# Pre-weighted exponentials and plain transposes in a sparse attention, and a convolution's first tap on the scalar engine

## The chip, the cores and the metric

The kernel runs on one core of a Trainium2 chip. The core has a matrix engine (TensorE, PE in the profile), a vector engine (VectorE, DVE), a scalar engine (ScalarE, ACT) and a general engine (GpSimd, POOL); a fifth (SyncE, SP) issues the weight loads. Each runs its own list of instructions in order and waits on semaphores that the others raise. On-chip data lie in SBUF; TensorE writes its products to eight PSUM banks, which VectorE and ScalarE read. The metric is the device time of one execution in microseconds; lower is better.

## The reference, cut to what matters

The program is three transformer blocks on 256 tokens of width 1024. The change touches the third, in two branches that are computed side by side. One is a sparse ("native sparse") attention of 16 heads in 4 groups, whose selection and window branches both become ordinary causal attention over the 256 tokens here:

```
s = einsum("bqgrd,bkgd->bgrqk", qb, kb) - slopes[:, :, None, None] * dist
p = jax.nn.softmax(jnp.where(mask, s, NEG), axis=-1)
return jnp.einsum("bgrqk,bkge->bqgre", p, vb)
o = gates[..., 0:1] * o_cmp + gates[..., 1:2] * o_slc + gates[..., 2:3] * o_win
```

The other is a gated delta rule, whose input first goes through a causal convolution of four taps and a SiLU:

```
qkv = jax.nn.silu(causal_depthwise_conv(qkv, conv_w))   # 3 * 1024 channels, 4 taps
q = l2norm(...); k = l2norm(...)
```

## The kernel before, in words

Each engine has its own program (`tensor_program`, `scalar_program`, `vector_program`, `gpsimd_program`), written as Python loops over the same steps. `Mark` counts what an engine has finished; `wait_ge(*dve.at("conv", j))` waits until VectorE has finished step conv of tile j. The order within an engine is the order of the code; no scheduler changes it.

Every weight is split in two float32r parts for accuracy: ScalarE copies 1024 columns to `whi` (L1394), VectorE subtracts to get `wlo` (L1913), and a 1024 x 128 product takes 24 matmuls (L567 to L569). The split runs at most three units ahead, in four buffers.

The stage of the change is the projection `f2`: 24 iterations s = 0 to 23, each giving one 128-channel tile j = F2[s] of queries, keys and values of the delta rule (16 tiles of keys and queries, which also need squares for the norms, and then 8 of values, j >= 16, which are transposed). In 17 of the 24 iterations (`STEPS2`) one turn of the sparse attention goes along. Of 16 turns in all, turns 0 and 1 have their scores before the stage; iterations 1, 2, 4, 5, 7, 8, 9, 11, 12, 14, 15, 16, 18 and 19 hold the scores of turns 2 to 15. These 14 are called head iterations below.

What each engine does in iteration s before the change, in its order:

- TensorE: the scores of turn i (L1051, `ns_scores`); the product of tile s (`product`), for which the PSUM bank of tile s-2 must be free and the `wlo` of unit s ready; column sums of squares (L585) or transposes of values (L1162) of tile s-2; then the turn i-2 (L1060, `ns_turn`) and the values of turn i-3 (L1074, L1082).
- ScalarE: `whi` of unit s+3; for value tiles the copies of the transposed tile (L1754); tanh of tile s-1 (L1763) after its convolution; the square of tile s-1 (L1768) after VectorE's `conv` of s-1; four exponentials of turn i (L1691) with their sums; two copies of the turned exponentials (L1699); on every second turn a copy of the output (L1705).
- VectorE: on a head iteration the reciprocal and gate of turn i-1 (L2345, L2347, `ns_weigh`), then the four maxima of turn i (L2334) and its bias (L2339); `wlo` of unit s+3 (L1913); `conv` of s-1, the SiLU's last factor (L2427); then the convolution of tile s, four operations from PSUM that each add one tap (L2436 the first, L2439 three more, each waiting for the one before); on every second turn a subtraction for the output (L2361).
- GpSimd: for each turn the product of the identity matrix with the four weights of each row (L2669), 128 x 512, in two buffers `dg2`.

The softmax weight (gate over sum) is applied in the turn itself: the exponentials are the stationary operand and the diagonal matrix of weights the moving one, so that the product is the transposed and weighted tile. These are float32 products. The other transposes of the kernel use TensorE's transpose with the identity.

Of the kernel before, what the change touches and what calls it, by code (L numbers as in the profile page):

```python
# [9 lines left out]
ALU = mybir.AluOpType  # L10
ACT = mybir.ActivationFunctionType
# [3 lines left out]
T = 256  # L15
# [293 lines left out]
STEPS2 = [(j + 1) * (N2 + 1) // 24 - j * (N2 + 1) // 24 for j in range(24)]  # L309

F2 = (*range(8, 16), *range(8), *range(16, 24))
CUTS = ((0, 128), (128, 384))
# [10 lines left out]
def program(nc, a):  # L323
    ctx = ExitStack()
    with ctx:
        area = [ctx]

        def sb(name, shape, dt=F32):
            return area[-1].enter_context(nc.sbuf_tensor("sb_" + name, shape, dt))
# [33 lines left out]
        sq = sb("sq", [128, KT, T])  # L363
# [83 lines left out]
        close()  # L447
        ss = sb("ss", [128, 3, 2, 384])
        pt2 = sb("pt2", [128, 2, 2, 384])
        dg2 = sb("dg2", [128, 2, 4, 128])  # L450
        nst = st[:, 0:64].rearrange("p (n k u t) -> p n k u t", n=4, k=4, u=2)
        close()
        scope()
# [30 lines left out]
        def C(name, lo=0, hi=None):  # L484
            s, e = COLS[name]
            return col[:, s + lo:(e if hi is None else s + hi)]
# [56 lines left out]
        def ps_of(step):  # L543
            return bank[bank_of.get(step, 0)]
# [7 lines left out]
        def tensor_program(te):  # L552
# [500 lines left out]

            def ns_turn(i):

                P.wait_ge(*pool.at("dg2", i))
                for u in range(2):
                    ps = take(RAS, ("npt", i, u), (act, ("npt", i, u)))
                    for k in range(3):
                        end = te.matmul(ps[:, k * 128:(k + 1) * 128], ss[:, i % 3, u, k * 128:(k + 1) * 128], dg2[:, i % 2, 2 * u + (k > 0), :], start=True, stop=True)  # L1060
                    end.then_inc(*pe.up(("npt", i, u)))

            def ns_values(i):
# [312 lines left out]
        def scalar_program(sc):  # L1376
# [306 lines left out]
            def attn_head(i):  # L1683
                if i < N2:
                    aa, r, _ = PAIRS2[i]
                    x = nst[:, i % 4, :, :, :]
                    A.wait_ge(*dve.at("nsneg", i))
                    for u in range(2):
                        for t, (lo, hi) in enumerate(CUTS):
                            p = ss[:, i % 3, u, lo:hi]  # L1690
                            sc.activation(p, p, ACT.Exp, bias=x[:, 1, u, t:t + 1], scale=slope((2 * aa + u) * 4 + r), accum_out=x[:, 2, u, t:t + 1]).then_inc(*act.up(("nsexp", i, u, t)))  # L1691

            def attn_tail(i):
                if 0 <= i - 2 < N2:
                    if i - 2 >= 2:
                        A.wait_ge(*pe.at("npv", i - 4))
                    for u in range(2):
                        A.wait_ge(*pe.at("npt", i - 2, u))
                        sc.activation(pt2[:, i % 2, u, :], ps_of(("npt", i - 2, u))[:, 0:384], ACT.Copy).then_inc(*act.up(("npt", i - 2, u)))  # L1699
                if 0 <= i - 3 < N2:  # L1700
                    aa, r, e = PAIRS2[i - 3]
                    j = aa * 4 + r
                    if e == 1:
                        A.wait_ge(*pe.at("npv", i - 3))
                        sc.activation(onh[:, j, :], ps_of(("no", j))[:, 0:T], ACT.Copy).then_inc(*act.up(("onh", j)))  # L1705
# [41 lines left out]
            def f2_later(s):  # L1747
# [11 lines left out]
                if 0 <= s - 1 < 24:  # L1759
# [4 lines left out]
                    if j < 16:  # L1764
# [2 lines left out]
                            A.wait_ge(*pe.at("qks", j // 2 * 2 + 9))  # L1767
                        sc.activation(sq[:, j % 8, :], src, ACT.Square).then_inc(*act.up(("qksq", j)))  # L1768

            step = 2  # L1770
            for s in range(24):
                weights("f2")
                f2_later(s)
                if STEPS2[s]:
                    attn_head(step)
                    attn_tail(step)
                    step += 1
            f2_later(24)
# [118 lines left out]
        def vector_program(ve):  # L1897
# [531 lines left out]
            def convolve(j):  # L2429
                dst = qk[:, j, :] if j < 16 else sq[:, j % 8, :]  # L2430
                ps = ps_of(("f2", j))
                wcol = C("conv", 4 * j, 4 * j + 4)
                V.wait_ge(*pe.at("f2", j))
                if j >= 16:
                    V.wait_ge(*pe.at("qks", (j - 16) // 2 * 2 + 1))
                ve.tensor_scalar(dst, ps[:, 0:T], wcol[:, 3:4], None, ALU.mult).then_inc(*dve.up())  # L2436
                for d in range(1, 4):
                    V.wait_ge(*dve.now())
                    ve.scalar_tensor_tensor(dst[:, d:T], ps[:, 0:T - d], wcol[:, 3 - d:4 - d], dst[:, d:T], ALU.mult, ALU.add).then_inc(*dve.up(*[("f2", j)] * (d == 3)))  # L2439

            step = 2
# [179 lines left out]
        def gpsimd_program(gp):  # L2621
            G = Waiter(gp)

            def regions(before):

                G.wait_ge(*pe.at(before))
                G.wait_ge(*act.at(before))
                G.wait_ge(*dve.at(before))

            def sums(norm):  # L2630

                for k in range(1, KT - 1):
                    G.wait_ge(*act.at("sq", norm, k))
                    if k > 1:
                        G.wait_ge(*pool.at("sum", norm, k - 1))
                    gp.tensor_tensor(sq[:, 0, :], sq[:, 0, :], sq[:, k, :], ALU.add).then_inc(*pool.up(("sum", norm, k)))  # L2636


            gp.memset(one, 1.0).then_inc(*pool.up("one"))
            for i in range(N0):  # L2640
                total = st[:, 64 + 2 * i:66 + 2 * i].unsqueeze(2).to_broadcast([128, 2, 128])
                G.wait_ge(*dve.at("w", i))
                if i == 0:
                    G.wait_ge(*dve.at("ctx", 7))
                if i > 1:
                    G.wait_ge(*pe.at("pt", i - 2, 1))
                gp.tensor_tensor(dg0[:, i % 2, :, :], ident.unsqueeze(1).to_broadcast([128, 2, 128]), total, ALU.mult).then_inc(*pool.up(("dg0", i)))
            for norm in ("ffn0", "mix1", "ffn1"):
                sums(norm)
            for k in range(1, KT - 1):  # L2650
                for norm, src in (("fin", sq), ("mix2", z8)):
                    G.wait_ge(*act.at("sq", norm, k))
                    if k > 1:
                        G.wait_ge(*pool.at("sum", norm, k - 1))
                    gp.tensor_tensor(src[:, 0, :], src[:, 0, :], src[:, k, :], ALU.add).then_inc(*pool.up(("sum", norm, k)))


            regions("block1")
            gp.memset(hvx[:, :, :, :], 0.0).then_inc(*pool.up("hvx"))
            gp.memset(bk[:, :, :], 0.0).then_inc(*pool.up("bk"))  # L2660
            gp.memset(pcs[:, :, :, :], 0.0).then_inc(*pool.up("pcs"))
            pool.note("f1")
            regions("f1")
            for i in range(N2):
                x = nst[:, i % 4, 3, :, :].rearrange("p u t -> p (u t)").unsqueeze(2).to_broadcast([128, 4, 128])
                G.wait_ge(*dve.at("nw", i))
                if i > 1:
                    G.wait_ge(*pe.at("npt", i - 2, 1))
                gp.tensor_tensor(dg2[:, i % 2, :, :], ident.unsqueeze(1).to_broadcast([128, 4, 128]), x, ALU.mult).then_inc(*pool.up(("dg2", i)))  # L2669
            pool.note("f2")  # L2670
            regions("f2")


            def decay(hd):
                G.wait_ge(*act.at("decay", hd))
                gp.tensor_tensor(Ebuf[:, hd % 2, :], Ebuf[:, hd % 2, :], K("mge"), ALU.mult).then_inc(*pool.up(("E", hd)))

            def level_mask(lv, n):
                msk = K("lev", lv * 64, lv * 64 + 64).unsqueeze(1).to_broadcast([128, 4, 64])
                G.wait_ge(*dve.at("W", 2 * n + 1))  # L2680
                if lv == 1:
                    G.wait_ge(*pe.at("first", n))
                    G.wait_ge(*dve.at("Y", 0, n))
                if lv > 1:
                    G.wait_ge(*pe.at("lup", lv - 1, n))
                gp.tensor_tensor(four(Wl, n), four(Wb, n)[:, :, 0:64], msk, ALU.mult).then_inc(*pool.up(("mask", lv, n)))

            G.wait_ge(s_con2, 16)
            for hd in range(8):
                decay(hd)  # L2690
            for n in range(4):
                level_mask(0, n)
            for n in range(4):
                level_mask(1, n)
            for lv, n in LEVELS:
                if lv < 5:
                    level_mask(lv + 1, n)
            G.wait_ge(*pool.now())
            gp.memset(Ys[64:128, :, 0:64], 0.0).then_inc(*pool.up("zeros"))
            pool.note("delta")  # L2700
            sums("mlp2")
# [276 lines left out]
```

## Time and profile before

| | us |
|---|---|
| median of 3 runs | 1182.01 (1180.71 to 1186.97) |
| the profiled execution's own time | 1183.51 |
| its span in the profile | 1181.7 |
| PE busy | 1138.0 (96% of the span) |
| DVE busy | 818.8 (69%) |
| ACT busy | 591.2 (50%) |
| POOL busy | 82.1 (7%) |

A busy time is the union of an engine's instructions. Matmuls are pipelined, one of 278 ns starting about 115 ns after the one before it, so a full TensorE shows as busy without gaps, and short gaps are hidden. For VectorE and ScalarE it is the start of each instruction that tells how the order moves on. The `f2` stage lies at about 660 to 796 us of the span.

### The profile page before, as it was taken

How to read it: one execution, taken by the hardware profiler on the slowest of the kernel's cores; microseconds unless marked ns; L12 is line 12 of the kernel's file. 1: busy time of each engine (PE TensorE's matmuls, PEld its weight loads, DVE VectorE, ACT ScalarE, POOL GpSimd, SP SyncE). 2: the span in 40 equal slices, each digit the busy share in tenths (PEclk: the TensorE clock that was granted, in tenths of full speed). 3: DMA queues.
4: the chain of work that ended last, by engine and by line, in shares of the span. 5: the costliest groups of instructions: out<-in, count | busy, mean ns of one | idle time of the engine just before them, and what ended most of it. 6: DMA issues, size and time to landing. Idle time of an engine off the chain costs nothing.

```text
span 1181.7 us, 23984 instructions
## 1 busy us (share of the span) xinstructions
PE 1138.0 (96%) x10258; PEld 1077.9 (91%) x10258; DVE 818.8 (69%) x1496; ACT 591.2 (50%) x1085; POOL 82.1 (7%) x101
## 2 busy tenths in 40 slices
PE   8888799999998999999999999999999999999999
PEld 2786799999997999999989988879999999999998
DVE  6776769988886776555765788879554665877443
ACT  2545555444435544554465657653224545665432
POOL 0000010000011000011100111113500001000000
PEclk9899999999999999999998999999999999999999
DMA  9732938888882567540742423222124555855520
GB/s 389 328 143 95 369 154 338 342 341 329 328 344 104 214 229 282 204 158 31 286 150 101 144 72 108 97 83 73 39 73 143 178 185 183 311 188 205 191 82 14
DMA packets 32220, 225.36 MB, mean 191 GB/s; under 512 B 3569, under 2 KB 4721, under 8 KB 5105
## 3 DMA queue, kind: packets, MB, share of 16 engines
q1 hardware_dynamic: 30530, 221.21, 49.9%
q10 hardware_dynamic: 1584, 2.62, 0.7%
q8 instruction: 81, 1.33, 0.4%
q14 instruction: 25, 0.20, 0.1%
HBM read 222.76 MB, written 1.05 MB: 189 GB/s over the span
## 4 chain that ended last, share of the span: by engine, by line
PE 87%; DVE 7%; ACT 4%; DMA 1%; issue 1%; POOL 0%; POOLq 0%; DVEq 0%
PE bank L567 23%; PE bank L569 23%; PE bank L568 23%; PE bank L1060 2%; PE bank L1051 1%; DVE sb_wlo L1913 1%; PE bank L585 1%; DVE sb_ring L1957 1%; PE bank L594 1%; PE bank L1082 1%; DVE sb_tmp L1942 1%; DMA sb_ring<-in_ada 1%; PE bank L1248 1%; ACT sb_whi L1394 1%; PE bank L1266 1%; PE bank L1262 1%
## 5 line engine op out<-in xcount | busy, mean ns | idle before, releaser
L567 PE MATMUL bank<-sb_xh,sb_whi 128*128 128x256 f32 x1480 | 418.5, 283 | 3.0 <-DVE sb_wlo L1913 2.7
L569 PE MATMUL bank<-sb_xh,sb_wlo 128*128 128x256 f32 x1480 | 411.1, 278 | 0.0
L568 PE MATMUL bank<-sb_xl,sb_whi 128*128 128x256 f32 x1480 | 411.0, 278 | 0.0
L1913 DVE TENSOR_TENSOR sb_wlo<-sb_ring,sb_whi 128x1024 fp32r<-128x1024 f32 x199 | 241.7, 1221 | 126.3 <-ACT sb_whi L1394 126.0
L567 PEld LDWEIGHTS bank<-sb_xh,sb_whi 128*128 128x128 f32 x1480 | 279.2, 189 | 10.8 <-issue 7.1
L568 PEld LDWEIGHTS bank<-sb_xl,sb_whi 128*128 128x128 f32 x1480 | 279.0, 189 | 0.1
L569 PEld LDWEIGHTS bank<-sb_xh,sb_wlo 128*128 128x128 f32 x1480 | 278.8, 188 | 0.0
L1394 ACT ACTIVATE sb_whi<-sb_ring 128x1024 fp32r<-128x1024 f32 x199 | 208.7, 1053 | 93.1 <-PE bank L569 79.5
L1913 DVE TENSOR_TENSOR sb_wlo<-sb_more,sb_whi 128x1024 fp32r<-128x1024 f32 x106 | 128.7, 1224 | 66.5 <-ACT sb_whi L1394 66.5
L567 PE MATMUL bank<-sb_hh,sb_whi 128*128 128x256 f32 x608 | 168.5, 277 | 0.0
L569 PE MATMUL bank<-sb_hh,sb_wlo 128*128 128x256 f32 x608 | 167.9, 276 | 0.0
L568 PE MATMUL bank<-sb_hl,sb_whi 128*128 128x256 f32 x608 | 167.9, 276 | 0.0
L1394 ACT ACTIVATE sb_whi<-sb_more 128x1024 fp32r<-128x1024 f32 x106 | 112.0, 1058 | 66.1 <-PE bank L569 56.1
L568 PEld LDWEIGHTS bank<-sb_hl,sb_whi 128*128 128x128 f32 x608 | 114.2, 188 | 0.0
L567 PEld LDWEIGHTS bank<-sb_hh,sb_whi 128*128 128x128 f32 x608 | 114.2, 188 | 0.0
L569 PEld LDWEIGHTS bank<-sb_hh,sb_wlo 128*128 128x128 f32 x608 | 114.1, 188 | 0.0
L1957 DVE CUSTOM_DVE_ANT_0 sb_ring<-sb_ring,sb_cB,sb_col 128x1024 f32<-128x1024 f32 x42 | 53.1, 1303 | 0.0
L1560 ACT ACTIVATE sb_tmp<-bank 128x256 f32<-128x256 f32 x44 | 16.9, 385 | 66.2 <-PE bank L569 66.1
L1416 ACT ACTIVATE sb_sq<-sb_h 128x256 f32<-128x256 f32 x48 | 19.2, 415 | 60.0 <-DVE sb_h L1971 55.2
L1957 DVE CUSTOM_DVE_ANT_0 sb_more<-sb_more,sb_cB,sb_col 128x1024 f32<-128x1024 f32 x38 | 47.7, 1293 | 0.0
L2636 POOL TENSOR_TENSOR sb_sq<-sb_sq 128x256 f32<-128x256 f32 x24 | 19.2, 802 | 365.3 <-ACT sb_sq L1416 364.4
L2669 POOL TENSOR_TENSOR sb_dg<-sb_con,sb_st 128x512 f32<-128x512 f32 x16 | 17.6, 1098 | 198.3 <-DVE sb_st L2347 109.4
(389 smaller groups left out, 1846.4 us busy)
## 6 DMA issues: line engine op xcount, KB each, us to landing
sb_more<-in_w SPq DMA_DIRECT2D x34, 1024.0 KB, 5.6
sb_ring<-in_w SPq DMA_DIRECT2D x32, 1024.0 KB, 5.7
sb_ring<-in_adaT SPq DMA_DIRECT2D x24, 1024.0 KB, 7.7
sb_ring<-in_f SPq DMA_DIRECT2D x22, 1024.0 KB, 4.9
sb_more<-in_adaT SPq DMA_DIRECT2D x20, 1024.0 KB, 8.7
sb_ring<-in_gn SPq DMA_DIRECT2D x8, 1024.0 KB, 4.9
sb_ring<-in_gd SPq DMA_DIRECT2D x8, 1024.0 KB, 4.9
sb_ring<-in_up SPq DMA_DIRECT2D x8, 1024.0 KB, 5.4
```

The costliest lines, as they stand in the source:

```text
L567: te.matmul(out, wh, rh, start=start, stop=False, skip_group_check=skip)
L568: te.matmul(out, wh, rl, start=False, stop=False, skip_group_check=skip)
L569: return te.matmul(out, wl, rh, start=False, stop=stop, skip_group_check=skip)
L585: end = te.matmul(out(t), src[:, c + t * 128:c + (t + 1) * 128], ones_, start=True, stop=True)
L1060: end = te.matmul(ps[:, k * 128:(k + 1) * 128], ss[:, i % 3, u, k * 128:(k + 1) * 128], dg2[:, i % 2, 2 * u + (k > 0), :], start=True, sto ...
L1394: sc.activation(hi, x, ACT.Copy).then_inc(*hi_done.up(n))
L1416: sc.activation(sq[:, k, :], src[:, k, :], ACT.Square).then_inc(*act.up(("sq", norm, k)))
L1560: sc.activation(temp(("silu", layer, j), (dve, ("hid", layer, j))), ps_of(("up", layer, j))[:, 0:T], ACT.Silu).then_inc(*act.up(("silu", l ...
L1913: ve.tensor_tensor(lo, x, hi.bitcast(F32), ALU.subtract).then_inc(*lo_dve.up(n))
L1957: ve.tensor_tensor_reduce(out=x, in0=x, in1=cB[:, 0, :], scale=1.0, scalar=C(f"ab{layer}", jj, jj + 1), op0=ALU.mult, op1=ALU.add, accum_o ...
L2636: gp.tensor_tensor(sq[:, 0, :], sq[:, 0, :], sq[:, k, :], ALU.add).then_inc(*pool.up(("sum", norm, k)))
L2669: gp.tensor_tensor(dg2[:, i % 2, :, :], ident.unsqueeze(1).to_broadcast([128, 4, 128]), x, ALU.mult).then_inc(*pool.up(("dg2", i)))
```

## The change: what it does

Three edits. GpSimd no longer builds the diagonal matrices: for each turn it multiplies the exponentials themselves by the weights, in place, in two instructions (128 x 2 x 128 and 128 x 2 x 256). TensorE's turn becomes plain transposes of the weighted exponentials, six per turn as before. And the first tap of the convolution is a scaled copy on ScalarE, placed between the exponentials of turn i and the copies of turn i-2; VectorE waits for it and adds the other three taps.

```diff
             def ns_turn(i):
 
-                P.wait_ge(*pool.at("dg2", i))
+                P.wait_ge(*pool.at("weighed", i))
...
-                        end = te.matmul(ps[:, k * 128:(k + 1) * 128], ss[:, i % 3, u, k * 128:(k + 1) * 128], dg2[:, i % 2, 2 * u + (k > 0), :], start=True, stop=True)
+                        end = te.transpose(ps[:, k * 128:(k + 1) * 128], ss[:, i % 3, u, k * 128:(k + 1) * 128], ident)
...
+            def first_tap(j):
+                dst = qk[:, j, :] if j < 16 else sq[:, j % 8, :]
+                A.wait_ge(*pe.at("f2", j))
+                if j >= 16:
+                    A.wait_ge(*pe.at("qks", (j - 16) // 2 * 2 + 1))
+                sc.activation(dst, ps_of(("f2", j))[:, 0:T], ACT.Copy, scale=C("conv", 4 * j + 3, 4 * j + 4)).then_inc(*act.up(("tap", j)))
+
             step = 2
-            for s in range(24):
+            for s, j in enumerate(F2):
                 weights("f2")
                 f2_later(s)
                 if STEPS2[s]:
                     attn_head(step)
+                first_tap(j)
+                if STEPS2[s]:
                     attn_tail(step)
                     step += 1
...
-                V.wait_ge(*pe.at("f2", j))
-                if j >= 16:
-                    V.wait_ge(*pe.at("qks", (j - 16) // 2 * 2 + 1))
-                ve.tensor_scalar(dst, ps[:, 0:T], wcol[:, 3:4], None, ALU.mult).then_inc(*dve.up())
+                V.wait_ge(*act.at("tap", j))
                 for d in range(1, 4):
-                    V.wait_ge(*dve.now())
+                    if d > 1:
+                        V.wait_ge(*dve.now())
...
             for i in range(N2):
-                x = nst[:, i % 4, 3, :, :].rearrange("p u t -> p (u t)").unsqueeze(2).to_broadcast([128, 4, 128])
                 G.wait_ge(*dve.at("nw", i))
-                if i > 1:
-                    G.wait_ge(*pe.at("npt", i - 2, 1))
-                gp.tensor_tensor(dg2[:, i % 2, :, :], ident.unsqueeze(1).to_broadcast([128, 4, 128]), x, ALU.mult).then_inc(*pool.up(("dg2", i)))
+                for t, (lo, hi) in enumerate(CUTS):
+                    p = ss[:, i % 3, :, lo:hi]
+                    x = nst[:, i % 4, 3, :, t].unsqueeze(2).to_broadcast([128, 2, hi - lo])
+                    gp.tensor_tensor(p, p, x, ALU.mult).then_inc(*pool.up(*[("weighed", i)] * t))
```

ScalarE in one head iteration before, from the tanh of the tile before to the copies of a turn (L1763 tanh, L1768 square, L1691 exponentials, L1699 copies, L1394 the weight split; s_dve and s_pe are the counts of VectorE and TensorE):

```order
L1763 ACTIVATE sb_tmp<-sb_qk 128x256 [waits s_dve]
L1768 ACTIVATE sb_sq<-sb_qk 128x256 [waits s_dve]
L1691 ACTIVATE sb_ss,sb_st<-sb_ss,sb_st 128x128
L1691 ACTIVATE sb_ss,sb_st<-sb_ss,sb_st 128x256
L1691 ACTIVATE sb_ss,sb_st<-sb_ss,sb_st 128x128
L1691 ACTIVATE sb_ss,sb_st<-sb_ss,sb_st 128x256
L1699 ACTIVATE sb_pt<-bank 128x384 [waits s_pe] x2
L1394 ACTIVATE sb_whi<-sb_ring 128x1024 [waits s_slot1]
```

And the same iteration now (line numbers of the changed kernel, one lower in this program; L1774 is the first tap):

```order
L1762 ACTIVATE sb_tmp<-sb_qk 128x256 [waits s_dve]
L1767 ACTIVATE sb_sq<-sb_qk 128x256 [waits s_dve]
L1690 ACTIVATE sb_ss,sb_st<-sb_ss,sb_st 128x128
L1690 ACTIVATE sb_ss,sb_st<-sb_ss,sb_st 128x256
L1690 ACTIVATE sb_ss,sb_st<-sb_ss,sb_st 128x128
L1690 ACTIVATE sb_ss,sb_st<-sb_ss,sb_st 128x256
L1774 ACTIVATE sb_qk<-bank,sb_col 128x256 [waits s_pe]
L1698 ACTIVATE sb_pt<-bank 128x384 [waits s_pe] x2
L1393 ACTIVATE sb_whi<-sb_ring 128x1024 [waits s_slot1]
```

The tap stands behind the square and the four exponentials of its iteration.

VectorE at the end of one iteration and the start of the next before, from the split (L1913) over `conv` (L2427) to the four taps (L2436, L2439):

```order
L1913 TENSOR_TENSOR sb_wlo<-sb_ring,sb_whi 128x1024 [waits s_hi]
L2427 SCALAR_TENSOR_TENSOR sb_qk<-sb_tmp,sb_qk 128x256 [waits s_act]
L2436 TENSOR_SCALAR sb_qk<-bank,sb_col 128x256 [waits s_pe]
L2439 SCALAR_TENSOR_TENSOR sb_qk<-bank,sb_col,sb_qk 128x255 [waits s_dve]
L2439 SCALAR_TENSOR_TENSOR sb_qk<-bank,sb_col,sb_qk 128x254 [waits s_dve]
L2439 SCALAR_TENSOR_TENSOR sb_qk<-bank,sb_col,sb_qk 128x253 [waits s_dve]
```

And now:

```order
L1921 TENSOR_TENSOR sb_wlo<-sb_ring,sb_whi 128x1024 [waits s_hi]
L2435 SCALAR_TENSOR_TENSOR sb_qk<-sb_tmp,sb_qk 128x256 [waits s_act]
L2445 SCALAR_TENSOR_TENSOR sb_qk<-bank,sb_col,sb_qk 128x255 [waits s_act]
L2445 SCALAR_TENSOR_TENSOR sb_qk<-bank,sb_col,sb_qk 128x254 [waits s_dve]
L2445 SCALAR_TENSOR_TENSOR sb_qk<-bank,sb_col,sb_qk 128x253 [waits s_dve]
```

One operation is gone, and the first that is left waits for ScalarE (s_act) where the removed one waited for TensorE (s_pe).

## Rows read from the trace of the kernel before

**Rows 1.** The page's busy times, with shares of the span

```profile
PE 1138.0 (96%) x10258; PEld 1077.9 (91%) x10258; DVE 818.8 (69%) x1496; ACT 591.2 (50%) x1085; POOL 82.1 (7%) x101
```

**Rows 2.** Chain that ended last, 660 to 800 us: start us, us, what

```profile
679.86 0.32 PE bank L567
...
682.80 1.34 PE bank L1060 x12
...
685.79 0.32 PE bank L567
...
760.42 0.32 PE bank L567
...
789.58 0.22 PE bank L1162 x2
```

**Rows 3.** Timeline of DVE: start us, us, instruction, [idle before <-releaser]

```profile
668.35 0.42 DVE L2427 SCALAR_TENSOR_TENSOR sb_qk<-sb_tmp,sb_qk 128x256 f32<-128x256 f32 x1
...
684.42 0.42 DVE L2427 SCALAR_TENSOR_TENSOR sb_qk<-sb_tmp,sb_qk 128x256 f32<-128x256 f32 x1
...
688.09 0.42 DVE L2361 TENSOR_TENSOR sb_onl<-bank,sb_onh 128x256 fp32r<-128x256 f32 x1 [1.30 <-ACT sb_onh L1705]
688.44 0.17 DVE L2345 RECIPROCAL sb_st<-sb_st 128x4 f32<-128x4 f32 x1
...
690.07 1.22 DVE L1913 TENSOR_TENSOR sb_wlo<-sb_ring,sb_whi 128x1024 fp32r<-128x1024 f32 x1
...
695.63 1.23 DVE L1913 TENSOR_TENSOR sb_wlo<-sb_ring,sb_whi 128x1024 fp32r<-128x1024 f32 x1 [1.99 <-ACT sb_whi L1394]
696.77 0.42 DVE L2427 SCALAR_TENSOR_TENSOR sb_qk<-sb_tmp,sb_qk 128x256 f32<-128x256 f32 x1
...
697.62 1.52 DVE L2439 SCALAR_TENSOR_TENSOR sb_qk<-bank,sb_col,sb_qk 128x255 f32<-128x255 f32 x3
699.05 0.17 DVE L2345 RECIPROCAL sb_st<-sb_st 128x4 f32<-128x4 f32 x1
...
759.70 0.41 DVE L2427 SCALAR_TENSOR_TENSOR sb_sq<-sb_tmp,sb_sq 128x256 f32<-128x256 f32 x1
```

**Rows 4.** Timeline of ACT, 684 to 688 us

```profile
684.88 0.42 ACT L1768 ACTIVATE sb_sq<-sb_qk 128x256 f32<-128x256 f32 x1 [2.64 <-DVE sb_qk L2427]
685.20 0.39 ACT L1691 ACTIVATE sb_ss<-sb_ss,sb_st 128x128 f32<-128x128 f32 x1
...
686.95 0.84 ACT L1699 ACTIVATE sb_pt<-bank 128x384 f32<-128x384 f32 x2
687.69 0.37 ACT L1705 ACTIVATE sb_onh<-bank 128x256 fp32r<-128x256 f32 x1
```

**Rows 5.** ACT groups by form, 600 to 900 us: busy us, mean ns of one

```profile
L1754 ACT ACTIVATE sb_vtm<-bank,sb_kroot 128x128 f32<-128x128 f32 x16 | 5.0, 363 | 16.5 <-PE bank L1162 16.5
...
L1662 ACT ACTIVATE sb_hrow<-bank 128x128 f32<-128x128 f32 x1 | 0.3, 277 | 2.5 <-PE bank L997 2.5
```

**Rows 6.** POOL groups by form: busy us, mean ns of one

```profile
L2669 POOL TENSOR_TENSOR sb_dg<-sb_con,sb_st 128x512 f32<-128x512 f32 x16 | 17.6, 1098 | 198.3 <-DVE sb_st L2347 109.4 <-PE bank L1037 89.0
L2676 POOL TENSOR_TENSOR sb_Msb<-sb_Msb,sb_con 128x384 f32<-128x384 f32 x8 | 8.1, 1018 | 32.7 <-ACT sb_Msb L1809 32.7
L2647 POOL TENSOR_TENSOR sb_dg<-sb_con,sb_st 128x256 f32<-128x256 f32 x8 | 4.9, 612 | 125.5 <-DVE sb_st L2056 125.5
```

**Rows 7.** Timelines of POOL (two rows) and DVE (one)

```profile
688.88 1.04 POOL L2669 TENSOR_TENSOR sb_dg<-sb_con,sb_st 128x512 f32<-128x512 f32 x1 [5.70 <-DVE sb_st L2347]
...
779.36 1.95 POOL L2669 TENSOR_TENSOR sb_dg<-sb_con,sb_st 128x512 f32<-128x512 f32 x1 [10.19 <-DVE sb_st L2347]
...
780.34 1.26 DVE L2427 SCALAR_TENSOR_TENSOR sb_sq<-sb_tmp,sb_sq 128x256 f32<-128x256 f32 x1
```

**Rows 8.** Timeline of PE, two transposes and the turn behind them

```profile
778.22 0.38 PE L1162 MATMUL bank<-sb_con,sb_sq 128*128 128x128 f32 x2
778.43 1.50 PE L1060 MATMUL bank<-sb_dg,sb_ss 128*128 128x128 f32 x12
```

**Rows 9.** Stretch of 10 us: stretch, busy us by engine, granted clock, DMA

```profile
640.00:650.00 10.00, 10.00 (x66) 9.20 (x65) 7.74 (x28) 5.59 (x13) 0.00 (x0) 0.66 0.01 2
```

More of the change, by code:

```diff
@@ L449, in program @@
         pt2 = sb("pt2", [128, 2, 2, 384])
-        dg2 = sb("dg2", [128, 2, 4, 128])
         nst = st[:, 0:64].rearrange("p (n k u t) -> p n k u t", n=4, k=4, u=2)
```

## The prediction

> **What bounds the kernel now.** I read the page first. TensorE is busy for 96% of the span, VectorE 69%, ScalarE 50%, GpSimd 7% [rows 1]: the reader sees one nearly full engine, and that anything given back by it is wanted. Then the chain that ended last, in the stretch of the change: it is TensorE nearly throughout, product after product. From the start of one product to the start of the next, in a head iteration without column sums or bias product, go 5.93 us (679.86 to 685.79), of which the turn has 1.34 [rows 2]. So the stage is bound by TensorE. But a full engine says nothing about how far behind it the others are. For that I read the timelines of VectorE and ScalarE and followed what each instruction waits for. `conv` of the first tile starts at 668.35 and that of tile 16 at 759.70 [rows 3]: 16 iterations, 12 of them head iterations, in 91.35 us. ScalarE's square waits for `conv` (2.64 us in the row shown) [rows 4], and VectorE's split waits 1.99 us for ScalarE [rows 3]. Both are slack today, but they show that the two engines already wait for each other once per iteration.
>
> **The turn on TensorE.** Six float32 products appear as 12 instructions and take 1.34 us in the chain [rows 2]. Two plain transposes start at 778.22 and the turn behind them at 778.43, so a transpose takes 0.105 us, one instruction each [rows 8]. Six are 0.65. The gain is 0.7 per turn, 11.2 us for 16 turns, if TensorE stays the last.
>
> **GpSimd.** Today one instruction of 128 x 512. Now 256 and 512 elements per partition, one after the other. The diagonal products of the same two sizes took 0.61 and, undisturbed, 1.04 us [rows 6, 7], together 1.65. The in-place product by a full table took 1.018 for 384 elements [rows 6], which in proportion is 2.04 for 768. That is 1.65 to 2.05; I take 1.7, because the new operation has, like the diagonal one, a dense operand and one that is repeated along the row. TensorE needs it an iteration later, so its own time is hidden. Its effect on VectorE is below.
>
> **The first tap, and the ring that it closes.** Until now VectorE's taps waited for TensorE alone. Now the tap of iteration s is on ScalarE, behind the square of tile s-1 and the four exponentials, and the square waits for VectorE's `conv` of s-1. So `conv`(s-1) -> square -> exponentials -> tap(s) -> three taps on VectorE -> weights, maxima and split of the next iteration -> `conv`(s) is a closed ring, with no work of VectorE beside ScalarE's part. Its pieces, from start to start:
> - `conv` to square 684.42 to 684.88, 0.46; square to the next 0.32; exponentials 685.20 to 686.95, 1.75 on head iterations [rows 3, 4].
> - Tap to VectorE: a copy of this size out of PSUM started at 687.69 and the VectorE instruction that waits for it at 688.09, 0.40 [rows 3, 4]. The tap also has a scale per partition: copies of 128 x 128 took 363 ns with one and 277 without [rows 5], so 0.09 more: 0.49. From below 0.40, from above 0.6.
> - Three taps to the next work, 697.62 to 699.05, 1.43. On every second turn the subtraction, 0.35 (688.09 to 688.44). On head iterations weights and maxima, 688.44 to 690.07, 1.63. Split to `conv`, 695.63 to 696.77, 1.14 [rows 3].
>
> A plain iteration is 0.46 + 0.32 + 0.49 + 1.43 + 1.14 = 3.84, a head iteration 1.75 + 1.63 more, 7.22. Over the same 16 iterations as above: 16 x 3.84 = 61.4; 12 blocks of exponentials 21.0; 11 blocks of weights and maxima 17.9; five subtractions 1.8; eight reads of sums and one small reciprocal, which I estimate at 0.9 from gaps of the same kind. Sum 103.0 against 91.35: 11.6 us more, although TensorE's own work fell to about 5.2 per such head iteration. TensorE cannot hide it, for it may be only two tiles ahead (two PSUM banks).
>
> After iteration 16 the ring opens, since value tiles have no square. TensorE is then the last again, and it arrives less late: from the product of tile 18 (760.42) to the end of that of tile 23 (789.58) are 29.16 us [rows 2], less four turns at 0.7, 26.4. In the kernel before this product began 0.7 after `conv`(16) (759.70); now TensorE waits for tile 16's taps, which end 1.2 before `conv`(16), so it begins some 1.1 before. From `conv`(16) to the end of product 23: 25.3 against 29.9, 4.6 us less. The ring alone is 11.6 - 4.6 = 7.0 us slower.
>
> **The port.** GpSimd's product started at 779.36 beside VectorE's split and took 1.95 instead of 1.04; VectorE's `conv` started at 780.34 and took 1.26 instead of 0.42 [rows 3, 7]. Each waited for the other's whole instruction. So far this was rare: GpSimd starts 0.44 after the reciprocal (688.44, 688.88) and is done at 1.48, before the split at 1.63. Now it is done at 0.44 + 1.7 = 2.14, and by the upper price at 2.5. The bias operation and the split, which stand just behind the maxima, wait at least 0.5 to 0.9; I take 0.6, since the small bias operation before the split waits too. Twelve times in the ring is 7.2, plus about 0.6 of waiting in iterations 19 to 21, where VectorE's lateness reaches TensorE: 7.8. The bounds are 0 (no collision, as with the maxima themselves, which read PSUM) and 12 x 0.95 + 1.5 = 12.9.
>
> The Trainium skill, SBUF — State Buffer, in its section on the two separate sides of SBUF, calls the port pair that VectorE and GpSimd share an exclusive lock held for the whole instruction, for VectorE instructions with two SBUF inputs. The row agrees (0.84 lost by `conv`). By that rule every head iteration must collide, where the rows alone, with one collision in 16 turns, would let one think it rare.
>
> **The sum.** 7.0 + 7.8 = 14.8 us on the profiled execution's 1183.5 (span 1181.7 and 1.8 around it), 1198.3. That execution is 1.5 above the median of the three runs. I say 1198.
>
> **Rivals.**
> - B, the ring is only partly on the path, or the port doesn't collide: 1183.5 + 7.0 = 1190.5 at most, and about 1184 where half of the ring's excess is also hidden. For it: fifteen of the sixteen products of GpSimd go undisturbed today (their mean of 1.098 is fifteen of 1.04 and the one of 1.95) [rows 6, 7]. Against it: they end 0.15 before the split, and the new pair will not.
> - C, faster: TensorE stays the last in every iteration, since ScalarE takes the tap early enough. Then the 11.2 of the turns are kept: 1172.3. It decides at a ring of under 5.2 us in a head iteration; I count 7.2. For it speaks that TensorE never idles now and VectorE loses 24 x 0.5 us of work. The Trainium skill, TensorE: Matmul & The Clock Gate, in its terms, calls the transpose mode four times faster for float32. The rows show 0.22 against 0.105, twice. By the page the turn would fall to 0.34, and this rival would give 1167.5.
> - D, the clock: with TensorE idle for a fifth of each ring, the granted clock may fall, as it did in the stretch 640 to 650 (0.66 on average, a mix of the levels 2.4 and 1.2 GHz) [rows 9]. At 1.2 GHz a head iteration's work of 5.2 to 5.9 is 10.4 to 11.8, above the ring's 7.8. If it falls in three of the twelve, 3 x 4 = 12 us more: 1210.
>
> **Numbers.** My forecast (ring and port, 1193 to 1206 by the bounds of tap and port) 0.64; B 0.20, C 0.07, D 0.09. A difference of 0.5% (5.9 us) is about what can be told from none: from 1176 to 1188 is "the same". Faster is C, 0.07. The same is 0.13 of B. Slower is the forecast, D and 0.07 of B, 0.80. The range 1186 to 1208 holds the forecast, half of B and part of D.
>
> **What would show it.** VectorE's first remaining tap waits for ScalarE, about 0.9 us in plain iterations and 2.7 in head iterations, some 36 us over the 16; ScalarE's square still waits for `conv`. `conv` to `conv` is 7.2 to 8.2 us in head iterations and 3.8 in plain ones, and 110 us in place of 91 over the 16. TensorE has gaps there and the chain passes through ScalarE and VectorE. The turn takes 0.65. GpSimd's second product ends after the split would have started, and the bias or the split shows a long duration. Wrong would be: a chain of TensorE alone in this stretch (C), GpSimd and VectorE overlapping without a lengthened instruction (B), or a clock under 1.00 in the stretch 660 to 790 (D).

## The result and the profile after

The kernel after takes 1198.61 us (median of six runs, 1194.9 to 1200.1), the kernel before 1183.16 beside it: 1.0121 times as long, with a 95% interval of 1.0096 to 1.0147. (This ratio, like the others below, is an estimate from all the runs of both kernels; the plain quotient of the two medians is 1.0131.) Forecast was 1198, slower.

The profiled execution has a span of 1198.1 us against 1181.7. First the page of the kernel after: its busy times, and the shares of the chain that ended last.

```profile
PE 1138.1 (95%) x10162; PEld 1073.8 (90%) x10162; DVE 812.4 (68%) x1472; ACT 599.5 (50%) x1109; POOL 91.4 (8%) x117
...
PE 76%; DVE 14%; ACT 8%; DMA 1%; issue 1%; POOL 0%; POOLq 0%; DVEq 0%; ACTq 0%
```

TensorE is as busy as before [rows 1], though it has 96 instructions fewer; in two stretches of the stage its matmuls ran at a lower granted clock (last row of the section on the prediction). The total doesn't show that something else took over, the chain does. Its shares were these before:

```profile
PE 87%; DVE 7%; ACT 4%; DMA 1%; issue 1%; POOL 0%; POOLq 0%; DVEq 0%
```

These pieces are from the chain of the kernel after, 668 to 778 us (start us, us, what), a stretch that held nothing but TensorE before:

```profile
687.07 0.56 DVE sb_st L2347
687.63 1.13 DVE sb_wlo L1921
...
689.55 1.76 ACT sb_ss L1690 x8
695.02 0.52 DVE sb_st L2347
...
697.53 1.75 ACT sb_ss L1690 x8
```

VectorE (bias, split), then ScalarE (exponentials), and so on around. The timeline of DVE shows the ring from VectorE's side, first and last row being `conv` of the first tile and of tile 16 (start us, us, instruction, [idle before <- releaser]):

```profile
669.37 0.41 DVE L2435 SCALAR_TENSOR_TENSOR sb_qk<-sb_tmp,sb_qk 128x256 f32<-128x256 f32 x1
...
688.69 0.41 DVE L2435 SCALAR_TENSOR_TENSOR sb_qk<-sb_tmp,sb_qk 128x256 f32<-128x256 f32 x1
691.70 1.51 DVE L2445 SCALAR_TENSOR_TENSOR sb_qk<-bank,sb_col,sb_qk 128x255 f32<-128x255 f32 x3 [2.60 <-ACT sb_qk L1774]
...
693.47 0.17 DVE L2353 RECIPROCAL sb_st<-sb_st 128x4 f32<-128x4 f32 x1
...
695.02 0.52 DVE L2347 TENSOR_TENSOR sb_st<-sb_st,sb_con 128x4 f32<-128x4 f32 x1
695.47 1.21 DVE L1921 TENSOR_TENSOR sb_wlo<-sb_ring,sb_whi 128x1024 fp32r<-128x1024 f32 x1
...
696.67 0.41 DVE L2435 SCALAR_TENSOR_TENSOR sb_qk<-sb_tmp,sb_qk 128x256 f32<-128x256 f32 x1
...
777.42 0.42 DVE L2435 SCALAR_TENSOR_TENSOR sb_sq<-sb_tmp,sb_sq 128x256 f32<-128x256 f32 x1
```

The 16 iterations from the first of these `conv` to the last take 108.05 us against 91.35 [rows 3]; one head iteration, 688.69 to 696.67, takes 7.98. ScalarE's side of the same iteration, in its timeline:

```profile
689.14 0.42 ACT L1767 ACTIVATE sb_sq<-sb_qk 128x256 f32<-128x256 f32 x1 [3.04 <-DVE sb_qk L2435]
689.46 0.39 ACT L1690 ACTIVATE sb_ss<-sb_ss,sb_st 128x128 f32<-128x128 f32 x1
...
691.22 0.45 ACT L1774 ACTIVATE sb_qk<-bank,sb_col 128x256 f32<-128x256 f32 x1
```

`conv` 688.69, square 689.14, exponentials 689.46, tap 691.22, the other taps 691.70: each starts when the one before it ends. VectorE stands still from `conv` to the taps (2.60), and ScalarE stood still before the square (3.04). Over 660 to 780 us the waits add up to this (us in total, times, longest us):

```profile
ACT sb_sq L1767 <- DVE sb_qk L2435: 40.7, 16, 3.4
DVE sb_qk L2445 <- ACT sb_qk L1774: 32.9, 16, 2.6
```

The first was 29.5 before (660 to 770 us), the second did not exist. GpSimd's two products and the turn, in the timeline of POOL and in the chain (a rare place where it passes over TensorE):

```profile
693.91 1.61 POOL L2675 TENSOR_TENSOR sb_ss<-sb_ss,sb_st 128x256 f32<-128x256 f32 x2 [6.30 <-DVE sb_st L2355]
```

```profile
740.08 0.67 PE bank L1059 x6
```

The products end at 695.52, and VectorE's bias operation, begun at 695.02, at 695.54: it took 0.52 where it took 0.16 in the kernel before (timeline of DVE, before). From the reciprocal to the split are 2.00 us against 1.63 in [rows 3], so 0.37 is lost per head iteration.

```profile
689.99 0.16 DVE L2339 TENSOR_TENSOR sb_st<-sb_st,sb_con 128x4 f32<-128x4 f32 x1
```

### The profile page after: what moved, and what is told of

The parts are those of the page before. It is cut to its first block, busy times and chain, and to the rows that moved or that the text cites. A ratio compares the mean times of both kernels' runs of the same rounds, so it can differ in the third digit from the quotient of the medians.

```text
span 1198.1 us, 23790 instructions
## 1 busy us (share of the span) xinstructions
PE 1138.1 (95%) x10162; PEld 1073.8 (90%) x10162; DVE 812.4 (68%) x1472; ACT 599.5 (50%) x1109; POOL 91.4 (8%) x117
## 4 chain that ended last, share of the span: by engine, by line
PE 76%; DVE 14%; ACT 8%; DMA 1%; issue 1%; POOL 0%; POOLq 0%; DVEq 0%; ACTq 0%
PE bank L566 21%; PE bank L567 21%; PE bank L568 21%; DVE sb_wlo L1921 3%; ACT sb_ss L1690 2%; DVE sb_ss L2342 1%; ACT sb_whi L1393 1%; DVE sb_qk L2445 1%; DVE sb_tmp L1950 1%; DVE sb_ring L1965 1%; DMA sb_ring<-in_ada 1%; PE bank L593 1%; PE bank L1247 1%; PE bank L1265 1%; PE bank L1261 1%
## 5 line engine op out<-in xcount | busy, mean ns | idle before, releaser
L2445 DVE SCALAR_TENSOR_TENSOR sb_qk<-bank,sb_col,sb_qk 128x255 f32<-128x255 f32 (+2 forms) x48 | 23.1, 482 | 34.0 <-ACT sb_qk L1774 32.9
```

## The experiments

All ratios are to the kernel before, run on the same chip, with their 95% interval. The second number is the time from `conv` of the first tile to `conv` of tile 16, from one profile each; it was 91.35 before and 108.05 after.

**The tap alone.** The kernel before with the third edit only: turn and GpSimd as they were.

```diff
+            def first_tap(j):   # on ScalarE, between exponentials and copies
-                ve.tensor_scalar(dst, ps[:, 0:T], wcol[:, 3:4], None, ALU.mult)...
+                V.wait_ge(*act.at("tap", j))
```

> The kernel before with the first tap on ScalarE as in the change; diagonal products on GpSimd and float32 turns on TensorE stay. Ring theory: the 16 iterations take 103 us in place of 91, none of it from the port; at the end of the stage 1.8 us come back: 1193 us, 1190 to 1196. Rival (the loss comes from the GpSimd edit): 1183 or a little less.

Measured: 1193.69 us, 1.0077 [1.0049, 1.0106], 104.04 us. The tap's place alone makes most of the loss.

**The other two edits alone.** The kernel after with the tap back on VectorE.

```diff
-                V.wait_ge(*act.at("tap", j))
+                V.wait_ge(*pe.at("f2", j))
+                ve.tensor_scalar(dst, ps[:, 0:T], wcol[:, 3:4], None, ALU.mult).then_inc(*dve.up())
```

> The changed kernel with the first tap back on VectorE, where it was; the in-place weights and the plain transposes stay. Ring theory (the tap behind the exponentials closes a ring with VectorE, and that alone is on the path): the ring is open, TensorE keeps the 0.7 us of each turn, VectorE's own head iteration is about 5.6 us with the port's share: 1175 us, 1171 to 1180. Rival (the in-place weights on GpSimd cost more than the transposes give): no faster than before, 1183 or more.

Measured: 1186.7 us, 1.0015 [0.9995, 1.0036], 95.20 us. A miss. The turn's 0.7 us were taken away and nothing came of it within the 16 iterations, which even take 3.85 longer. The chain of this kernel in the stretch still passes over the two other engines (start us, us, what):

```profile
684.32 0.42 ACT sb_sq L1767
684.74 1.76 ACT sb_ss L1690 x8
686.49 0.75 ACT sb_pt L1698 x2
687.24 0.28 ACT sb_onh L1704
...
687.54 0.42 DVE sb_onl L2360
...
689.96 1.13 DVE sb_wlo L1912
...
691.16 0.34 DVE sb_qk L2426
...
691.53 0.42 ACT sb_sq L1767
```

This is a ring without a tap: square, exponentials, the two copies, the copy `onh`, VectorE's subtraction and its weights and maxima, split, `conv`, square. In iterations without `onh` it goes on over the copy `whi`, for which the split waits. VectorE's two waits in it are those of the kernel before, 1.30 for `onh` and 1.99 for `whi` [rows 3].

**The tap ahead of ScalarE's wait for `conv`.**

```diff
             def f2_later(s):
+                if s < 24:
+                    first_tap(F2[s])      # ahead of tanh, the wait for conv, and the square
```

> The changed kernel with the tap of tile s placed ahead of ScalarE's wait for conv of tile s-1, so ahead of the square and the exponentials. ScalarE does the same instructions. Ring theory: VectorE no longer waits for ScalarE's square and exponentials, its own work is 0.5 us per iteration less: 1173 us, 1168 to 1179. Rival (it is the hand-over from ScalarE to VectorE, or ScalarE's added 11 us of work, that costs): 1190 or more.

Measured: 1182.78 us, 0.9986 [0.9964, 1.0009], 93.73 us. Also a miss: the loss is gone, but the expected gain isn't there either.

**The tap between square and exponentials.**

```diff
+                first_tap(j)
                 if STEPS2[s]:
                     attn_head(step)
-                first_tap(j)
```

> The changed kernel with the tap between the square and the exponentials. Ring theory: the ring stays closed but loses the 12 blocks of exponentials of 1.75 us, so conv to conv over 16 iterations falls from 108 to 87 us, VectorE waits 0.9 us in every iteration: 1179 us, 1175 to 1184. Rival (the place within ScalarE does not matter): 1198.

Measured: 1191.13 us, 1.0049 [1.0025, 1.0073], 101.17 us. Slower than expected, a miss too. Over 660 to 780 us VectorE waits for the tap only 0.85 us an iteration, 13.6 in all, but the tap lengthens what ScalarE does between `conv` and the split by some 0.36 to 0.42 each time; 16 times that is the 6.0 us by which this run's 101.17 exceed the 95.20 of the run with the tap on VectorE. The waits of the older ring stay:

```profile
ACT sb_sq L1767 <- DVE sb_qk L2434: 33.7, 16, 3.1
DVE sb_qk L2444 <- ACT sb_qk L1774: 13.6, 16, 0.9
```

**GpSimd's products held back,** until VectorE's `conv` of the iteration; tap and turn as in the kernel after.

```diff
+                if i > 0:
+                    G.wait_ge(*dve.at("conv", F2[heads[i - 1] - 1]))
```

> The changed kernel; GpSimd starts each in-place product only after VectorE's conv of that iteration, so that it runs beside the taps, which read PSUM and one SBUF operand. Port theory: VectorE's bias operation is back to 0.16 us, 12 x 0.37 us leave the ring: 4 to 5.5 us less than the changed kernel, 1194. Rival (the bias operation is longer for another reason, or its length is not on the path): 1198.6 as the changed kernel.

Measured: 1193.84 us, 1.0095 [1.0073, 1.0117], 104.05 us: as with the tap alone. The collisions cost 108.05 - 104.05 = 4.0 us over the 16 iterations, eleven times 0.37.

**Longer work on GpSimd behind the products:** a further product with two operands read, 128 x 512 (first diff), or a memset of 128 x 1024, which reads nothing (second).

```diff
+                gp.tensor_tensor(dg2[:, i % 2, :, :], ident.unsqueeze(1).to_broadcast([128, 4, 128]), x4, ALU.mult)...
```

```diff
+                gp.memset(dg2[:, :, :, :], 0.0)...
```

> The changed kernel with one more GpSimd product per turn behind the two, the old diagonal one of 128 x 512, whose result nobody reads. Port theory: it holds the port 1.04 us longer in every head iteration, VectorE's bias or split waits so much longer: 12 x 1.04 and about 1 at the end, 13.5 more than the changed kernel, 1212 (1208 to 1215). If the port is given to VectorE in between, the split goes first and conv waits instead, for about the same. Rival (GpSimd and VectorE don't hinder each other): 1198.6.

> The changed kernel with a GpSimd memset of 128 x 1024 behind the two products, about 0.95 us, which writes SBUF and reads nothing. If only reading holds VectorE's two-operand instructions up: 1198.6 as the changed kernel. If any GpSimd instruction does: 12 x 0.95, 1210.

Measured: 1209.32 us, 1.0217 [1.0189, 1.0245], 117.58 us with the product; 1198.37 us, 1.0129 [1.0102, 1.0155], 108.07 us with the memset. In the timelines of POOL and DVE of the run with the extra product, `conv` takes 1.26 where it has 0.42 of work, and ends 0.28 after GpSimd's instruction:

```profile
688.89 2.10 POOL L2680 TENSOR_TENSOR sb_dg<-sb_con,sb_st 128x512 f32<-128x512 f32 x1
```

```profile
690.01 1.26 DVE L2436 SCALAR_TENSOR_TENSOR sb_qk<-sb_tmp,sb_qk 128x256 f32<-128x256 f32 x1
```

GpSimd waits out the split of 688.88 to 690.09 first (2.10 for a product of 1.04), then `conv` waits out GpSimd. The memset runs beside the split, and neither is lengthened (0.95 and 1.21); `conv` begins after it and has its usual length:

```profile
687.66 0.95 POOL L2679 MEMSET sb_dg<- 128x1024 f32 x1
```

```profile
687.66 1.21 DVE L1922 TENSOR_TENSOR sb_wlo<-sb_ring,sb_whi 128x1024 fp32r<-128x1024 f32 x1
688.80 0.41 DVE L2436 SCALAR_TENSOR_TENSOR sb_qk<-sb_tmp,sb_qk 128x256 f32<-128x256 f32 x1
```

So a busy GpSimd alone does not hold VectorE up: the product that reads SBUF does, the memset that only writes it does not. No run has a GpSimd instruction of the same kind in both forms. The Trainium skill, SBUF — State Buffer, section on the two separate sides, says the same: the lock binds a VectorE instruction with two SBUF inputs only against a GpSimd instruction that reads SBUF. Both runs agree.

**The older ring.** The misses left one question: what holds the 91 us once the tap's ring is open? My theory by then: before the change two bounds were equally long, TensorE and the ring without a tap. On ScalarE the square is the only instruction of that ring that waits for `conv`. Moved behind the exponentials and copies, it no longer stands between `conv` and what VectorE waits for, `onh` and `whi` (second diff). Four kernels: tap on VectorE and GpSimd held back (first diff on top of the second experiment); the kernel before with the square moved and nothing else; both together; and both together with the tap first on ScalarE.

```diff
+                if i > 0:
+                    G.wait_ge(*dve.at("conv", F2[heads[i - 1] - 1]))
```

```diff
-                        sc.activation(sq[:, j % 8, :], src, ACT.Square)...     # in f2_later(s)
                 f2_later(s)
                 if STEPS2[s]:
                     attn_head(step)
                     attn_tail(step)
                     step += 1
+                f2_square(s)          # the wait for conv of s-1, then the square
```

> The kernel after with the tap back on VectorE and, besides, GpSimd's product held back until VectorE's conv of its iteration. The first such run, without the hold, came to 1.0015 of the kernel before, with 95.2 us over the 16 iterations instead of 91.35. My present theory: before, an older ring (conv, square, exponentials, copies, VectorE's splits, conv) was as long as TensorE's work, so that the transposes' gain is lost on it and only GpSimd's collisions (0.37 a head iteration, 4 us) were added. Then this run is at 91 to 91.5 over the 16 iterations and 1180 to 1184. Rival: the remaining 3.9 us have another cause than the collisions; then it stays at 95 and 1186. Third: the transposes' gain shows once the collisions are gone, 83 and 1172.

> The kernel before with ScalarE's square of a tile moved from ahead of the exponentials to the end of its iteration, behind the copies; nothing else. My theory: before, the old ring and TensorE tie. With the square last the exponentials no longer wait for conv, the old ring is open, but TensorE still needs 91 us for the 16 iterations: 1181 to 1184, the same, with ScalarE's waits for conv gone from ahead of the exponentials and VectorE's waits for ScalarE (1.99 at the high cast) smaller. Rival: TensorE was not a bound at all there and the ring alone was; then this is faster, 1176 or less.

> Transposes, tap on VectorE, GpSimd's product late, and the square last: TensorE's work of the 16 iterations is 12 turns x 0.68 = 8 us less and no ring should hold it. Theory (a tie of two bounds before): the gain appears only here, 83 to 86 us over the 16 iterations and 1172 to 1176, though the square's move alone and the transposes alone each give nothing. Rival: a third bound stands close behind (VectorE's or ScalarE's own work); then 88 to 91 and 1178 to 1183.

> As the one with both rings open, but the tap is on ScalarE, ahead of everything that waits for conv: the change as it might have been made. VectorE has 0.5 us less per iteration, ScalarE 0.46 more. By the theory 83 to 85 us over the 16 iterations and 1171 to 1174, no worse than with the tap on VectorE; if VectorE's own work is the next bound, 2 to 4 us better than it; if ScalarE's is, worse than it (1178).

| | ratio to before | 16 iterations, us |
|---|---|---|
| transposes, GpSimd late, square as it was | 0.9973 [0.9957, 0.9989] | 91.77 |
| kernel before, square last | 0.9997 [0.9981, 1.0013] | 91.43 |
| transposes, GpSimd late, square last | 0.9902 [0.9878, 0.9926] | 82.35 |
| the same, tap first on ScalarE | 0.9908 [0.9893, 0.9922] | 82.44 |

The theory holds. Moving the square gives nothing to the kernel before, though it shortens the waits: ScalarE's square waited 29.5 us for `conv` there, and in the second kernel of the table (waits, 660 to 770 us) 8.1, with another 11.1 of the exponentials for the bias. Its chain stays with TensorE:

```profile
ACT sb_ss L1691 <- DVE sb_st L2344: 11.1, 11, 1.7
ACT sb_sq L1771 <- DVE sb_qk L2432: 8.1, 4, 3.1
```

```profile
683.75 1.34 PE bank L1060 x12
685.09 0.80 PE bank L1082 x8
```

The transposes give nothing within the 16 iterations while the ring stands, and 9.0 us of the 91.35 when it is cut. The 0.27% of the first kernel comes from behind the ring: `conv` 16 to `conv` 23 takes 31.53 there against 35.05. The third kernel's chain is TensorE's again, with the short turn, and TensorE shows no gap between 680 and 760 us (stretch, busy us by engine, granted clock, DMA):

```profile
697.39 0.71 PE bank L1059 x6
698.10 0.80 PE bank L1081 x8
698.90 0.86 PE bank L1050 x8
```

```profile
680.00:700.00 20.00, 20.00 (x175) 17.04 (x175) 18.89 (x62) 14.30 (x44) 4.84 (x6) 1.00 0.30 106
```

Where the tap stands makes no difference then (0.9902 and 0.9908): the expected 2 to 4 us for a freer VectorE would come only if VectorE were next, and TensorE is still last. The first kernel of the table shows the ring by itself. Two of its iterations, from the `conv` at 686.65 to that at 698.99, take 12.34 us, and the same two take 12.35 in the kernel before (684.42 to 696.77, [rows 3]), though each turn of TensorE now takes 0.7 less. In 690 to 700 us its granted clock is 0.66, a mix of the two levels, and there the chain passes over TensorE for once, 691.68 to 699.71: a product's steps come every 0.21 us where they came every 0.12, and the eight of L1081 take 1.48 for 0.80.

```profile
693.51 1.48 PE bank L1081 x8
...
695.50 0.21 PE bank L567
```

What this cost VectorE stands in its timeline, in the wait of its first tap:

```profile
686.65 0.42 DVE L2426 SCALAR_TENSOR_TENSOR sb_qk<-sb_tmp,sb_qk 128x256 f32<-128x256 f32 x1
...
698.99 0.42 DVE L2426 SCALAR_TENSOR_TENSOR sb_qk<-sb_tmp,sb_qk 128x256 f32<-128x256 f32 x1
699.73 0.48 DVE L2435 TENSOR_SCALAR sb_qk<-bank,sb_col 128x256 f32<-128x256 f32 x1 [0.32 <-PE bank L568]
```

From 698.99 to the next `conv` are 5.50 us against 5.08 in the kernel before. The other fifteen of the 16 iterations have the length that they have in the kernel before, within 0.02. So 0.42 of the 91.77 are the clock's, and the ring alone takes 91.35, as long as the 91.43 that TensorE alone takes in the second kernel. The run without GpSimd's hold has 95.20; the 3.4 us between the two are the collisions.

**The kernel after, square last.** One move, tap and GpSimd as the change has them.

```diff
                 if STEPS2[s]:
                     attn_tail(step)
                     step += 1
+                f2_square(s)
```

> The kernel after with the square alone moved to the end of its iteration; tap on ScalarE behind the exponentials, and GpSimd's product where the change put it. The ring of the prediction went from conv through the square to the exponentials and the tap; without that step a shorter one is left: tap, 0.48 to the taps, 1.43, weights, maxima and bias 1.6 to 2.0 (with GpSimd's collision), exponentials 1.76, tap: 5.3 to 5.7 us in a head iteration, against TensorE's 5.2. I expect 85 to 90 us over the 16 iterations in place of 108, and 1176 to 1181. Rival: the ring is not closed by the square but by another wait, say by GpSimd's slower product on the maxima's bias; then it stays above 100 us and 1190.

Measured: 1175.28 us, 0.9924 [0.9895, 0.9952], 84.93 us, slightly better than expected. Against the kernel after this is 23 us less over the 16 iterations, for one instruction with its wait that stands a few places later. VectorE's wait for the tap falls from 32.9 to 10.2 us (waits, 660 to 770 us):

```profile
DVE sb_qk L2450 <- ACT sb_qk L1777: 10.2, 12, 1.7
```

The shorter ring that I expected is there, in its chain: from bias to bias 5.79 us in an iteration without subtraction. It holds the 16 iterations 2.6 us above the 82.35 of TensorE alone:

```profile
705.71 0.53 DVE sb_st L2352
706.26 1.86 ACT sb_ss L1690 x8
708.12 0.37 ACT sb_qk L1777
...
708.51 0.49 DVE sb_qk L2450
...
711.50 0.53 DVE sb_st L2352
```

GpSimd's collision is still in it (0.53 for the bias). All three kernels with transposes and the square last beat both the kernel before and the kernel after; their intervals don't tell them apart.

## Why the prediction was right, and which step of it was not

- **The forecast's mechanism** held: the tap closes the ring, VectorE waits 32.9 us for it (forecast some 36, with 0.85 plain and 2.60 head against 0.9 and 2.7), the 16 iterations take 108 (forecast 110), and the chain runs over ScalarE and VectorE. Rival B is answered by this: the ring's excess is not half hidden but on the path in full, and the port does collide, eleven times in the 16 iterations. The run with the tap alone shows the ring as its cause: 104.04 against my 103.0. Each plain iteration behind a head one was 0.17 longer than counted, since the split waits for `whi` there (timeline of DVE, kernel after).

```profile
701.37 1.23 DVE L1921 TENSOR_TENSOR sb_wlo<-sb_ring,sb_whi 128x1024 fp32r<-128x1024 f32 x1 [0.17 <-ACT sb_whi L1393]
```

- **The sum** was 7.0 + 7.8 = 14.8, measured 14.3 (0.0121 of 1183). Two terms were mis-sized and made up for each other, so that the sum came out this near is in part luck. The ring without collisions, by the runs, costs 0.0095 of 1183, 11.2 us, in place of 7.0: it was 1.0 longer than counted, and later iterations gave less back (in the kernel with GpSimd held back `conv` 16 to `conv` 23 took 31.3 against 35.05 before, 3.7 in place of 4.6); the remaining 2 us or so lie within what the interval of that ratio leaves open. The port costs 0.0121 - 0.0095, some 3 us by two ratios whose intervals overlap, 4.0 by the two profiles over the 16 iterations and 0.5 behind them, in place of 7.8: I took 0.6 twelve times where eleven times 0.37 is right, since only the small bias operation waits, and only for what is left of GpSimd's second product.
- **The durations** were right: turn 0.67 (0.65), GpSimd's products 1.61 (1.7), tap to VectorE 0.48 (0.49).
- **The step that failed** did not carry the forecast, but rival C: "So the stage is bound by TensorE", and the waits of ScalarE and VectorE for each other "are slack today". They were not. In [rows 3] the two `conv` at 684.42 and 696.77 are 12.35 apart, and the products of TensorE that start at 679.86 and 685.79 [rows 2] are followed by one at 692.35 in the same chain, which is 12.49. That these are nearly equal would be so in any case, since engines that wait for each other keep step. What tells is whether a link of the ring waits for TensorE, and none does: the square starts 0.46 after `conv`, exponentials and copies follow without a gap [rows 4], VectorE waits 1.30 for `onh` and 1.99 for `whi` [rows 3], all on the ring itself. TensorE has no gap either. So the two bounds ran level, and the runs with one of them taken away confirm it, 91.43 without the ring and 91.35 without TensorE's part (91.77 less 0.42). The chain names only one of two equal bounds. So rival C's rule, that below 5.2 us for the tap's ring the 11.2 us of the turns are kept, was wrong: with that ring open, the two runs were at 1.0015 and 0.9986. Only with the older ring cut as well was the gain there, 0.9902, and in that kernel it is nearly what C had put down (11.2 of 1183 would be 0.9905).
- **Rival D**, the clock: it did fall, as the timeline in stretches of 20 us of the kernel after shows, once around 690 and once around 750.

```profile
680.00:700.00 20.00, 17.75 (x122) 14.89 (x122) 13.43 (x41) 11.75 (x35) 3.22 (x4) 0.83 0.21 78
```

  But my price of 4 us a time rested on a TensorE that then becomes the last. The chain stayed with the ring in both stretches. The runs with the tap alone and with GpSimd held back had clocks of 1.00 and 0.86 over 680 to 700 us and took 104.04 and 104.05 for the 16 iterations. In the kernel with GpSimd held back and the tap on VectorE the fall lay on the chain for 8 us and cost 0.42.

## What to carry to other kernels

When an in-order engine waits for another in the middle of its list, everything behind that wait that the other engine needs joins a ring; before putting work there, write the ring down from start to start and compare it with the bound, and put the wait, with what needs it, last in the list instead. A chain of waits over one engine does not say that the others have slack: follow each closed ring from link to link in the timelines before counting a saving on the engine named. If no link waits for that engine, as here over 12.35 us, the ring has no slack. The period that is seen says nothing, since coupled engines show the same one. Two bounds that run level need both edits: here each alone gave 0.3% at most, both together 1% (with GpSimd's product held back, or 0.8% without that and with the tap on ScalarE).

## What the runs showed of the hardware

- A GpSimd product that reads SBUF stopped a VectorE instruction with two SBUF inputs for its whole rest (`conv` 1.26 in place of 0.42) and itself waited for the split before it (2.10 in place of 1.04). A memset of 0.95 us beside the split lengthened nothing (1.21).
- Two in-place products with a repeated factor, 256 and 512 elements per partition, took 1.61 us on GpSimd together.
- The granted clock fell to a mix of its two levels in stretches where TensorE had gaps (0.83 over 680 to 700 us, busy 17.75 of 20). Gaps alone don't explain it: in the same kernel 720 to 740 us had more of them (busy 16.26) at 1.00, and 640 to 660 us of the kernel before had 0.83 with a busy time of 20.00. At 1.2 GHz a product's steps come every 0.21 us in place of 0.12. What that costs depends on whether TensorE is on the chain at that moment: nothing was seen of it in the ring of the tap, and 0.42 us in the older one.
